# Attention heads in pairs of KV groups, and the fifth modulation vector on four column groups of TensorE

## The reference, cut to what matters

```
m = silu(cvec) @ w_mod[l] + b_mod[l]        # six vectors of 1024: sh1, sc1, g1, sh2, sc2, g2
h = rms_norm(x, n1) * (1 + sc1) + sh1
q, k, v, u = split(h @ w_in)                # 8 query heads, 2 key/value heads of 64, conv input
q, k = rms_norm(q), rms_norm(k)             # latent tiles also get rotary angles
s = q k^T / sqrt(64);  p = softmax(s);  attn = p v
conv = silu(layer_norm(depthwise_conv31(a * sigmoid(b)) + bias))
x = x + g1 * (concat(attn, conv) @ w_out)
h2 = rms_norm(x, n2) * (1 + sc2) + sh2
x = x + g2 * grouped_moe(h2)                # 16 experts, the best 2 of one group
```

## Time and profile before

| | us |
|---|---|
| median of 3 runs | 1123.59 (1122.86 to 1124.43) |
| span of the profiled execution | 1121.9 |
| PE busy | 982.3 (88%) |
| DVE busy | 404.9 (36%) |
| ACT busy | 157.1 (14%) |
| POOL busy | 123.3 (11%) |
| SP's main queue, share of 16 DMA engines | 61.6% |

### The profile page before, as it was taken

One profiled execution on the slowest core, in us unless ns is written; L12 is line 12 of the kernel. 1 busy time (PEld: TensorE's weight loads), 2 busy tenths in 40 slices (PEclk: granted clock), 3 DMA queues, 4 the chain that ended last, 5 costly groups with the idle time before them and its releaser, 6 DMA issues. The chain is left out here.

```text
span 1121.9 us, 12453 instructions
## 1 busy us (share of the span) xinstructions
PE 982.3 (88%) x4812; PEld 467.2 (42%) x4812; DVE 404.9 (36%) x902; ACT 157.1 (14%) x364; POOL 123.3 (11%) x188
## 2 busy tenths in 40 slices
PE   4799999997898989988799979999678997889886
PEld 2555545454333333333266544554523333333332
DVE  0189855245211110111435994533521111011206
ACT  1101233220000000000130014422000000000010
POOL 1001200511000000000221020060200000000010
PEclk9899889997999999988799997999579999999988
DMA  9928973368999996999950475225965999999932
GB/s 339 383 95 310 302 298 108 124 219 355 424 420 425 425 367 272 422 427 421 360 220 24 150 270 223 76 92 185 362 234 220 415 426 425 423 424 422 420 134 75
DMA packets 64570, 328.59 MB, mean 293 GB/s; under 512 B 7448, under 2 KB 10184, under 8 KB 48084
## 3 DMA queue, kind: packets, MB, share of 16 engines
q1 hardware_dynamic: 44224, 277.89, 61.6%
q0 software_dynamic: 9072, 27.89, 6.8%
q10 hardware_dynamic: 11172, 21.42, 5.8%
HBM read 305.88 MB, written 21.30 MB: 292 GB/s over the span
## 5 line engine op out<-in xcount | busy, mean ns | idle before, releaser
L1782 PE MATMUL ps<-big 128*64 128x512 f32 x1024 | 244.6, 630 | 27.6 <-issue 11.9
L1798 PE MATMUL ps<-big,scr 128*64 128x512 f32 x624 | 156.3, 644 | 5.6 <-DVE scr L1428 4.3
L1477 PE MATMUL ps<-big 128*128 128x384 f32 (+2 forms) x448 | 147.9, 492 | 5.1 <-ACT big L786 5.1
L1782 PEld LDWEIGHTS ps<-big 128*64 128x64 f32 x1024 | 78.5, 144 | 173.1 <-issue 159.5
L1124 DVE SCALAR_TENSOR_TENSOR scr<-scr,convw 128x384 f32<-128x384 f32 x240 | 134.1, 613 | 2.3
L1441 DVE TENSOR_TENSOR scr<-ps,scr 128x256 f32<-128x256 f32 x32 | 13.6, 424 | 278.2 <-ACT scr L953 278.1
L1477 PEld LDWEIGHTS ps<-big 128*128 128x128 f32 x448 | 86.0, 193 | 64.7 <-issue 24.8
L1798 PEld LDWEIGHTS ps<-big,scr 128*64 128x64 f32 x624 | 50.6, 148 | 97.9 <-issue 96.9
L1698 PE MATMUL ps<-big 128*128 128x512 f32 x192 | 84.4, 594 | 1.4 <-ACT big L826 1.4
L1493 PE MATMUL ps<-big,cs_rep 128*32 128x256 f32 x640 | 49.5, 466 | 14.4 <-DMA big<-in_w_mod_dram 14.4
L953 ACT ACTIVATE scr<-ps 128x256 f32<-128x256 f32 x32 | 12.3, 383 | 325.2 <-PE ps L1782 325.2
(11 more groups left out here) (231 smaller groups left out, 842.5 us busy)
## 6 DMA issues: line engine op xcount, KB each, us to landing
big<-in_w_gate_dram SPq DMA_DIRECT2D x32, 2048.0 KB, 18.4
big<-in_w_up_dram SPq DMA_DIRECT2D x32, 2048.0 KB, 22.8
big<-in_w_down_dram SPq DMA_DIRECT2D x32, 2048.0 KB, 18.9
big<-in_w_mod_dram SPq DMA_DIRECT2D x23, 2048.0 KB, 15.3
big<-in_w_in_dram SPq DMA_DIRECT2D x6, 2048.0 KB, 23.5
expert_rows<-scr ACTq DMA_DIRECT2D x68, 128.0 KB, 8.5
big<-in_w_out_dram SPq DMA_DIRECT2D x4, 2048.0 KB, 19.8
expert_rows<-x ACTq DMA_DIRECT2D x1, 7168.0 KB, 42.6
```

The lines of the kernel that those rows point to most:

```text
L1477: mm = pe.matmul(out, stationary(k), moving(k), start=(k == 0), stop=(k == n - 1))
L1782: mm = pe.matmul(ps[b * TT:(b + 1) * TT, bank, :].rearrange("p (m n) -> p m n", m=2), tokens(k), w[:, :, k, b * HF:(b + 1) * HF], start=(k ...
L1798: mm = pe.matmul(ps[b * TT:(b + 1) * TT, bank, :], src[:, k % 2 * P + k // 2 * TT:k % 2 * P + (k // 2 + 1) * TT], w[:, k, b * SEG:(b + 1) ...
```

## The change

A unit u = 3j + t (12 a layer) now holds query heads j and 4 + j of tile t. Their scores go to rows 0 to 63 and 64 to 127 of the array and to two banks (`SCORE_BANK`); one maximum and one reciprocal on DVE cover both; ACT does two exps; POOL multiplies prob by the inverse sums (`share`) before PE transposes it; ACT copies both heads' probT at once; in the weighted values v is stationary (64 columns a head, the two heads on two column groups) and probT moves, so that the output is already transposed: ACT copies it to hT (`take_attention`), and `head_output` and the first three mix_transposed are gone. w_out's rows for attention are loaded in the order (g, d) by j, in two DMAs beside one for the conv rows. Scores of unit u + 2 are issued behind the transposes of unit u. The taps are dealt out by `UNIT_TAPS`.

Vector 4 is made by `vector` (four column groups of 32), one step in each of units 1 to 8, taken by DVE at u = 9 with b_mod and norm2_g in lanes. POOL's waits and stores for gateB move into its units 1 and 5. In the layer norm DVE also applies gain and bias, and POOL keeps the inverse deviation and the last product. Banks (`out_bank`, `BACK`, `LOGITS`) and waits follow; before the transposes of the last experts' marks, PE has one more wait, on ov_taken.

```diff
-EARLY_TAPS, ROPE_TAPS, BETWEEN_TAPS, LATE_TAPS, HEAD_TAPS = 80, 6, 0, 0, 5
+EARLY_TAPS, ROPE_TAPS, BETWEEN_TAPS, LATE_TAPS = 80, 6, 0, 0
+UNIT_TAPS = [1, 4, 4, 1, 4, 4, 1, 4, 3, 0, 0, 0]
...
-HEAD_FILL = [(8 + hd // 4, hd % 4 * (KD // 4), (hd % 4 + 1) * (KD // 4)) for hd in range(HEADS)]
+UNIT_FILL = [0, 1, 1, 1, 1, 1, 1, 1, 1, 0, 0, 0]
+assert sum(UNIT_FILL) == KD
...
-        prob = scr[:, 0:TILES * 384].rearrange("p (t n) -> p t n", t=TILES)
-        probT = scr[:, TILES * 384:2 * TILES * 384].rearrange("p (t n) -> p t n", t=TILES)
+        prob, probT = (scr[:, n * 4 * 384:(n + 1) * 4 * 384].rearrange("p (b g n) -> p b g n", b=2, g=KV_HEADS)
+                       for n in range(2))
...
-                    load(("out", l, n), w_out_v[l, :, :, n * SEG:(n + 1) * SEG])
+                    item, cols = ("out", l, n), slice(n * SEG, (n + 1) * SEG)
+                    s = slot_of(item)
+                    if past(uses(item) - 1):
+                        sp.wait_ge(slot_used[s], uses(item) - 1)
+                    for g_ in range(KV_HEADS):
+                        sp.dma_start(slot_w(s)[g_ * HD:(g_ + 1) * HD, 0:PAIRS, :], w_out_heads[l, g_, :, :, cols])\
+                            .then_inc(slot_loaded[s], 16)
+                    sp.dma_start(slot_w(s)[:, PAIRS:KD, :], w_out_v[l, :, :, cols]).then_inc(slot_loaded[s], 16)
...
+                def share(u):
+
+                    n = P * len(KEY_CHUNKS[u % TILES])
+                    p_ = prob[:, u % 2, :, 0:n]
+                    pool.wait_ge(rinv_ready, l * UNITS + u + 1)
+                    g.tensor_tensor(p_, p_, stats(RI + 2 * (u % 2), 2).unsqueeze(2).broadcast_to([P, 2, n]), ALU.mult)\
+                        .then_inc(prob_ready, 1)
+
+                for u in range(UNITS):
+                    share(u)
+                    if u == 1:
+                        pool.wait_ge(mod_taken, taken_at(l, 2))
+                        lane_out(pool, mod_dram[:, 2 * D:3 * D], rowC, modC_st)
+                    if u == 5:
+                        pool.wait_ge(modC_st, (l + 1) * LANES * 16)
+                        spread(gateB[:, :, :], 2, bcG_in)
 
                 pool.wait_ge(mod_done, l + 1)
+                lane_out(pool, mod_dram[:, 3 * D:5 * D], rowB, modB_st)
+                for t in range(TILES):
+                    pool.wait_ge(ln_var, l * 3 + t + 1)
+                    rstd(stats(LNR + t), stats(LNV + 2 * t + 1), 1, 1.0, EPS).then_inc(ln_rstd, 1)
                 pool.wait_ge(cache_st, l * 32 + 32)
 
 
+                for t in range(TILES):
                     pool.wait_ge(ln_sig, l * 3 + t + 1)
                     g.tensor_tensor(h[:, t, CH:D], h[:, t, CH:D], sg, ALU.mult).then_inc(mix_ready, 1)
...
+                def softmax(u):
+
+                    n = P * len(KEY_CHUNKS[u % TILES])
+                    act.wait_ge(nmax, l * UNITS + u + 1)
+                    for g_ in range(KV_HEADS):
+                        at = 2 * (u % 2) + g_
+                        ins = a.activation(prob[:, u % 2, g_, 0:n], ps[:, SCORE_BANK[u % 2] + g_, 0:n], ACT.Exp,
+                                           bias=stats(NM + at), accum_out=stats(RS + at))
+                    ins.then_inc(exp_done, 1)
+
+                def take_probT(u):
+                    n = P * len(KEY_CHUNKS[u % TILES])
+                    act.wait_ge(t_ps, l * UNITS + u + 1)
+                    a.copy(probT[:, u % 2, :, 0:n], ps[:, 1:3, 0:n]).then_inc(probT_ready, 1)
+
+                def take_attention(j):
+
+                    act.wait_ge(o_ps, l * PAIRS + j + 1)
+                    a.copy(hT_all[:, :, j, :], by_seg(ps[:, 7, 0:CAP])).then_inc(attn_out, 1)
+
+                softmax(0)
+                for u in range(UNITS):
+                    if u + 1 < UNITS:
+                        softmax(u + 1)
+                    take_probT(u)
+                    if u and u % TILES == 0:
+                        take_attention(u // TILES - 1)
+                take_attention(PAIRS - 1)
...
+                if c == 4:
+                    dve.wait_ge(gain_in, (l + 1) * LANES * 16)
...
+                row = (rowC, rowB[:, 0:LW], rowB[:, LW:2 * LW], rowG)[c - 2]
+                v.tensor_tensor(row, ps[:, bank, 0:LW], row, ALU.add).then_inc(mod_taken, 1)
+                if c == 4:
                     dve.wait_ge(mod_taken, taken_at(l, c))
-                    ins = v.scalar_tensor_tensor(row, row, 1.0, gain, ALU.add, ALU.mult)
-                    if c != 8:
-                        ins.then_inc(mod_done, 1)
+                    v.scalar_tensor_tensor(row, row, 1.0, gain_row, ALU.add, ALU.mult).then_inc(mod_done, 1)
...
+                def score_max(u):
+
+                    at, n = SCORE_BANK[u % 2], P * len(KEY_CHUNKS[u % TILES])
+                    dve.wait_ge(s_ps, l * UNITS + u + 1)
+                    v.tensor_reduce(stats(NM + 2 * (u % 2), 2), ps[:, at:at + 2, 0:n], AX.X, ALU.max, negate=True)\
+                        .then_inc(nmax, 1)
+
+                def inverse_sum(u):
+
+                    at = 2 * (u % 2)
+                    dve.wait_ge(exp_done, l * UNITS + u + 1)
+                    v.reciprocal(stats(RI + at, 2), stats(RS + at, 2)).then_inc(rinv_ready, 1)
 
                 def ln_stats(t):
                     dve.wait_ge(back_ps, l * 3 + t + 1)
+                    if past(l * 3 + t):
+                        dve.wait_ge(ln_var, l * 3 + t)
                     step.link(v.bn_stats(stats(BN, 6), ps[:, BACK[t], :]))
+                    v.bn_aggr(stats(LNV + 2 * t, 2), stats(BN, 6)).then_inc(ln_var, 1)
 
                 def ln_normalize(t):
+
+                    z = h[:, t, CH:D]
+                    if t == 0:
+                        dve.wait_ge(ln_in, (l + 1) * 32)
+                    dve.wait_ge(ln_var, l * 3 + t + 1)
+                    step.link(v.scalar_tensor_tensor(z, ps[:, BACK[t], :], stats(LNV + 2 * t), lnB[:, 0, :],
+                                                     ALU.subtract, ALU.mult))
                     dve.wait_ge(ln_rstd, l * 3 + t + 1)
+                    v.scalar_tensor_tensor(z, z, stats(LNR + t), lnB[:, 1, :], ALU.mult, ALU.add).then_inc(ln_out, 1)
...
                 score_max(0)
+                score_max(1)
+                for u in range(UNITS):
+                    if u:
+                        if u + 1 < UNITS:
+                            score_max(u + 1)
+                    taps(UNIT_TAPS[u])
+                    inverse_sum(u)
+                    if u == 9:
+                        mod_take(l, 4)
+                for t in range(TILES):
+                    ln_stats(t)
+                for t in range(TILES):
+                    ln_normalize(t)
...
+            def unit_fill(l, u):
+
+                k0 = sum(UNIT_FILL[:u])
+                if u == UNIT_FILL.index(1):
+                    pe.wait_ge(mod_taken, taken_at(l, 3))
+                vector(l, 4, k0, k0 + UNIT_FILL[u])
...
+                def scores(u):
+                    j, t = divmod(u, TILES)
                     ks = KEY_CHUNKS[t]
+                    for g_ in range(KV_HEADS):
+                        rows = slice(g_ * HD, (g_ + 1) * HD)
+                        mm = pe.matmul(ps[:, SCORE_BANK[u % 2] + g_, 0:P * len(ks)], qT[rows, t, j * P:(j + 1) * P],
+                                       kT[rows, ks[0] * P:(ks[-1] + 1) * P], start=True, stop=True)
+                    mm.then_inc(s_ps, 1)
+
+                def prob_transposed(u):
+                    for g_ in range(KV_HEADS):
+                        for n in range(len(KEY_CHUNKS[u % TILES])):
+                            mm = pe.transpose(ps[:, 1 + g_, n * P:(n + 1) * P], prob[:, u % 2, g_, n * P:(n + 1) * P], ident)
+                    mm.then_inc(t_ps, 1)
+
+                def weighted_values(u):
+                    j, t = divmod(u, TILES)
+                    ks = KEY_CHUNKS[t]
+                    pe.wait_ge(probT_ready, l * UNITS + u + 1)
+                    if t == 0 and past(l * PAIRS + j):
+                        pe.wait_ge(attn_out, l * PAIRS + j)
+                    for n, c_ in enumerate(ks):
+                        for g_ in range(KV_HEADS):
+                            mm = pe.matmul(ps[g_ * HD:(g_ + 1) * HD, 7, (TILES - 1 - t) * P:(TILES - t) * P],
+                                           vall[:, c_, g_ * HD:(g_ + 1) * HD], probT[:, u % 2, g_, n * P:(n + 1) * P],
+                                           start=(n == 0), stop=(n == len(ks) - 1))
+                    if t == TILES - 1:
+                        mm.then_inc(o_ps, 1)
...
+                scores(0)
+                scores(1)
+                for u in range(UNITS):
+                    pe.wait_ge(prob_ready, l * UNITS + u + 1)
+                    if u == 0:
+                        pe.wait_ge(mod_taken, taken_at(l, 3))
+                    else:
+                        pe.wait_ge(probT_ready, l * UNITS + u)
+                    prob_transposed(u)
+                    if u + 2 < UNITS:
```

(97 more changed lines are left out.)

173 lines of the change are left out of this document (31 added, 142 removed).

## The result

The changed kernel takes 1142.24 us (median of 4 runs, 1137.88 to 1144.69) where the kernel before, run beside it, takes 1124.01 (4 runs): ratio 1.0165, 95% interval 1.0116 to 1.0215. It is 18 us slower; the forecast was 43 us slower. In the profiled executions (spans 1136.0 and 1121.9) the stages read as follows, cut at the same instructions.

A forecast was written before the change was run, and what follows sets the result against it. TensorE's own work bounded the attention stage before; after, a serial loop through five engines at half clock would. Stage +19.8 us, per layer +21.9, two layers 43.8 on 1123.6: about 1167 us, range 1128 to 1184.

The forecast's parts named there:

- The loop: Attention stage: each unit passes serially through the engines, no overlap between units' loops; 81.1 us where 61.3 stood.
- Rival 2: Attention stage: the loop does not bind, the busiest engine sets the time; 1074 us; chance 0.04, its mild form 0.04.
- rival 3: Paired scores on TensorE: row groups do not overlap; 15.8 us a layer more, 1198 us; chance 0.06.
- the tail: From the last reciprocal to project_out: multiplication, transposes, values and ACT's copy, 7.8 us at half clock.
- I take 1.2 GHz for the whole stage and until project_out has run a while.: TensorE's clock in the attention stage: half throughout, lacking 512-column passes and with some 2 us idle per 7 us unit.
- start at half clock: Beginning of project_out: 3.5 us extra because TensorE's clock would still be at half there.
- clock back for half the units: Attention stage: the case between half and full clock, about 1149 us; chance 0.17.
- POOL's product: Multiplication of probabilities by inverse sums in the loop: 1.9 us for 768 elements, 0.65 for 256, scaled by size.
- The crossings between engines: Three handovers between engines in each unit's loop: 0.1 us each, 0.3 together, bounds 0.1 and 0.6.
- the taps in the loop: DVE's taps inside the loop, 25 of 26: 15.1 us a layer, at 0.54 or 0.64 each.
- a term put at nothing: Values and fill on TensorE within the loop: costed at nothing, as hidden by taps and POOL.
- It passes on whole: After the attention stages: later loads wait for slots freed as much later, so the delay reaches the end, 43.8 us.

The follow-up runs named there:

- e1: The changed kernel with DVE taking the reciprocal of unit u before its taps and the maximum of u + 2 behind them; 1114.59 us, ratio 0.9942.
- e6: The changed kernel with DVE's order maximum(u + 1), taps(u), reciprocal(u + 1), the reciprocal of unit 0 first; 1097.07 us, ratio 0.979.
- e2: The kernel before, heads unpaired, with only vector 4 on four column groups of 32, one step a head; 1156.68 us, ratio 1.0303.
- e5: e2 with two unread 256-column matmuls a head behind the fill of heads 0 to 6; 1116.20 us, ratio 0.9974 to the kernel before.
- e8: The changed kernel, pairs kept, with vector 4's old fill in two rows of 512 columns, two steps in units 1 to 8; 1150.37 us, ratio 1.0276.
- e3: The changed kernel with POOL's product cut to the first column of each head's probabilities; 1104.38 us, ratio 0.9839.

## Why the prediction was right and wrong

**Right: the mechanism and the sign.** The loop binds, as the rows after and e1 show. It runs through three engines, though (DVE, POOL, TensorE), and not the five that the prediction's heading has: in the loop of layer 0 DVE waits for ACT only at the last reciprocal, 1.42 us. DVE waits for TensorE 2.1 to 4.8 us ahead of each maximum of units 3 to 10. Rival 2 (the loop does not bind) is out; a form of it became true only when e6 reordered DVE.

**Right: row groups overlap.** Four 384-column passes of a pair take 0.85 us at full clock and 1.58 at half, where 0.84 and 1.6 were taken; rival 3 is out. TensorE's timeline after, at full clock:

```profile
159.25 0.44 PE L1634 MATMUL ps<-table_sb,scr 128*128 128x128 f32 x2 [0.21 <-POOL scr L625]
159.61 0.92 PE L1627 MATMUL ps<-scr 64*128 64x384 f32 x4
160.46 0.88 PE L1645 MATMUL ps<-scr 128*64 128x128 f32 x12
```

The change is 18 us where 43 were forecast. A layer came out 12.5 and 13.1 us shorter than forecast: in layer 0, 10.0 in the loop, 2.1 in the tail and 0.4 behind them.

**Wrong: the step on the clock, the largest part of it.** "I take 1.2 GHz for the whole stage and until project_out has run a while." It was 0.72 on average; passes at the full rate stand at 154, at 158 to 162, at 179 to 181 and at 185, and from 196 on all are. By its terms, loop, first score to last reciprocal (136.68 to 200.01): 63.3 us for 73.3. Transposes, scores and the crossing to the maximum, for the ten steps of its sum, by start of transposes to start of maximum: 21.5, of which the forecast had 25.5 without the crossing: 4.0 less at least. In the tail, from the last reciprocal to project_out, the transposes took 0.8 for 1.6, and the whole 5.7 for 7.8. And project_out needed no start at half clock (3.5): its first 24 passes took 10.41 to the next start. Waits that I had not counted took most of that back in layer 0: 0.67 and 0.68 for ACT's copies inside project_out, and 1.36 for DVE ahead of h2_transposed(0). So 39.2 against 39.6 is two errors that cancel, and layer 1 has 37.6. The case "clock back for half the units", 1149, which had 0.17, was the better description. The reasoning failed where it let one property (no 512-column pass) decide alone. e2 has no such pass and stays at 0.50, but e5 has none either and runs at the full clock; in the changed kernel, with short passes and holes, the clock came back several times, and in e8, with 512-column passes, it fell at about 167.8, within the hole of 6.01.

**Wrong: POOL's product.** Taken at 1.9 by size; it took 1.47 (768 elements) and 0.61 (256), so 2.8 us less in the loop of a layer. The lower bound, 1.27, was nearer. The two sizes give an estimate of 0.18 us and 1.68 ns an element, 1.04 us for 512, where a product of two full operands takes 1.27: the step that failed is the scaling from that product, for with the broadcast operand it came out cheaper and not dearer.

**Smaller terms.** The crossings between engines were 0.05 to 0.08 for 0.1 each; the maximum (0.96 and 0.42 for 0.95 and 0.4) hands over to the taps at 0.88 and 0.34; the taps in the loop came to 14.6 for 15.1; the first reciprocal to 3.65 for 4.2; a reciprocal took 0.16 for 0.2. Together these make about the other 3.2 of the loop's 10.0 us. Against them stands a term put at nothing: in step 10 the transposes began 0.64 behind the product (196.05 for 195.41), behind the values and the fill on TensorE. "It passes on whole" held in the medians: the stages of both layers differ by 18.5 us together from before, the medians by 18.2. The spans of the profiled executions differ by 14.1 only, as what follows h2_transposed(0) in layer 1 took 343.1 for 348.3; no single execution shows the delay whole.

**What the forecast did not see.** It found the loop and priced it, but did not ask what a change of DVE's order alone would be worth, though its own terms gave it: the taps (15 us a layer) lay in the loop only because the reciprocal was queued behind them.

## What to carry to other kernels

Where units pass through several engines in turn, write down for each engine what its queue holds between receiving and releasing; work that nobody waits for (here the taps) belongs behind the release. Moving the taps there gave 27.6 us over two layers (e1), and moving the next maximum behind the next reciprocal as well 42.5 (e6), without removing an instruction. Do not count saved columns on TensorE as saved time before knowing the clock that remains: shortening the fill by 0.8 us a head cost 3.3 us a head. When a clock cannot be forecast, price the stage at both levels and centre between them instead of taking one for all of it.

## What the runs showed of the hardware

**Busy time alone does not give the clock.** In e2 TensorE was busy for 50.00 of 50.00 us at 0.50; with 0.97 us more of 256-column passes a head (e5) its passes ran at the full rate from 149 on, just as busy. "TensorE: Matmul & The Clock Gate" of the Trainium skill, Part 1, says that the gate follows how busy the engine has recently been; if that is the busy time of these records, e2 does not fit it, and the measurement decides. What tells e2 and e5 apart for the gate, no run here separates.

**Taps and product slow each other.** Groups by line, from 137 to 185: of e3, where there is no product to speak of, and of e1, where it lies beside the taps:

```profile
L1132 DVE SCALAR_TENSOR_TENSOR scr<-scr,convw 128x384 f32<-128x384 f32 x26 | 15.5, 614 | 0.4
```

```profile
L1131 DVE SCALAR_TENSOR_TENSOR scr<-scr,convw 128x384 f32<-128x384 f32 x26 | 22.1, 869 | 0.4
L625 POOL TENSOR_TENSOR scr<-scr,stat 128x768 f32<-128x768 f32 x7 | 12.0, 1718 | 17.9 <-DVE stat L1216 17.9
```

A tap takes 614 ns alone and 869 on average beside the product, a large product 1.47 us alone and 1.76 beside the taps: 6.6 us of DVE's time in e1 (22.1 less 15.5), and part of the reason why e6, with the maximum first (781 ns a tap), is faster still. In e6 the large products keep their 1.47 us: they begin beside the maximum, ahead of the taps, and only the taps are slowed. In e1 they begin behind the first tap and take 0.29 more, the small ones 0.30 more (0.91 for 0.61). "GPSIMD Engine Reference" of the Trainium skill, section "Specifications", says that GPSIMD shares its SBUF interfaces with VectorE and contends with VectorE's instructions of two SBUF inputs; these traces agree, in both directions in e1 and in one in e6.
